# A recurrence whose response part runs ahead of its scan, and a gate product through split parts, on one core

## The reference, cut to what matters

```python
def step(x, u_blk):                      # of s5_scan; complex state x, 64 states in each of 64 groups
    bu = jnp.einsum('btgh,gph->btgp', u_blk.astype(jnp.complex64), b_bar)
    bu = bu.at[:, 0].add(a_bar * x)
    a = jnp.broadcast_to(a_bar, bu.shape)
    _, xs = lax.associative_scan(_affine_compose, (a, bu), axis=1)
    y = jnp.einsum('btgp,ghp->btgh', xs, c_mat).real
    return xs[:, -1], y
...
def s5_out(y, u, d_skip, w_glu, dtype):
    b, t = u.shape[:2]
    y = (y + d_skip.astype(jnp.float32).reshape(S5_GROUPS, S5_GROUP) * u).reshape(b, t, D_MODEL)
    z = jax.nn.gelu(y).astype(dtype) @ w_glu
    za, zb = jnp.split(z, 2, axis=-1)
    return za * jax.nn.sigmoid(zb)
...
    y_lf, _ = s5_scan(u_l, ab_f, bb_f, c_f, x_cf)
    y_lb, _ = s5_scan(u_l[:, ::-1], ab_b, bb_b, c_b, x_cb)
    out_l = s5_out(y_lf + y_lb[:, ::-1], u_l, d_skip, w_glu, h_l.dtype)
```

## Time and profile before

| | |
|---|---|
| median of 3 runs | 2630.1 us (2624.09, 2630.1, 2630.54) |
| profiled execution | 2623.83 us, span 2622.0 us, granted clock 0.962 |
| busy in the span | PE 2353.7 (90%), PEld 1857.2 (71%), DVE 1478.4 (56%), ACT 1035.9 (40%), POOL 210.2 (8%) |
| chain that ended last | PE 73%, DVE 14%, ACT 7%, DMA 3% |
| recurrence, from the norm's root to the first gate matmul | 2162 to 2356.4 |
| gate product | 2356.4 to 2413.5 |
| last norm, to the last MLP's first matmul | 2413.5 to 2429.7 |

### The profile page before, as it was taken

One profiled execution on the slowest core, in us unless ns is written; L12 is line 12 of the kernel. 1 busy time (PEld: TensorE's weight loads), 2 busy tenths in 40 slices (PEclk: granted clock), 3 DMA queues, 4 the chain that ended last, 5 costly groups with the idle time before them and its releaser, 6 DMA issues.

```text
span 2622.0 us, 35101 instructions
## 1 busy us (share of the span) xinstructions
PE 2353.7 (90%) x14706; PEld 1857.2 (71%) x14706; DVE 1478.4 (56%) x2327; ACT 1035.9 (40%) x1742; POOL 210.2 (8%) x294
## 2 busy tenths in 40 slices
PE   5987788999997988888997988989999998978999
PEld 2854365888884766667996853357788778757999
DVE  5337656556555377875455235546566545871454
ACT  3243444222234355554444335544322324221543
POOL 0001200000000033320000002200201100000110
PEclk8988999999998999998998999999999998989999
DMA  7145552434421455334552323423444332352453
GB/s 265 65 162 201 227 191 68 159 137 151 152 89 65 140 181 161 129 129 138 189 185 83 105 92 131 171 110 120 137 153 150 122 147 103 130 187 95 161 180 126
DMA packets 174846, 372.78 MB, mean 142 GB/s; under 512 B 8384, under 2 KB 101824, under 8 KB 160480
## 3 DMA queue, kind: packets, MB, share of 16 engines
q1 hardware_dynamic: 174688, 370.53, 40.3%
HBM read 340.07 MB, written 30.44 MB: 141 GB/s over the span
## 4 chain that ended last, share of the span: by engine, by line
PE 73%; DVE 14%; ACT 7%; DMA 3%; issue 2%; POOL 0%; SPq 0%; DVEq 0%; ACTq 0%
PE ps L169 72%; DVE sb_R L200 5%; ACT sb_R L248 2%; DMA sb_R<-mod_w 1%; DVE sb_R L232 1%; DVE sb_WP L200 1%; DMA sb_slot<-mod_w 1%; DVE sb_H L200 1%; PE ps L179 1%; DVE sb_cst L214 1%; DVE sb_X L217 1%; DVE sb_R L229 1%; DVE sb_cst L200 1%; ACT L244 1%; ACT sb_R L254 1%
## 5 line engine op out<-in xcount | busy, mean ns | idle before, releaser
L169 PE MATMUL ps<-sb_HP,sb_WP 128*128 128x512 f32 (+1 forms) x5736 | 1087.8, 351 | 48.6 <-DVE sb_WP L200 24.6
L169 PEld LDWEIGHTS ps<-sb_HP,sb_WP 128*128 128x128 f32 x5736 | 923.4, 192 | 196.9 <-DVE sb_HP L200 22.7
L200 DVE TENSOR_TENSOR sb_WP<-sb_slot,sb_WP 128x1024 fp32r<-128x1024 f32 x364 | 449.5, 1240 | 650.9 <-ACT sb_WP L254 650.7
L254 ACT ACTIVATE sb_WP<-sb_slot 128x1024 fp32r<-128x1024 f32 x364 | 383.0, 1057 | 788.9 <-PE ps L169 774.0
L169 PE MATMUL ps<-sb_XP,sb_WP 128*128 128x512 f32 (+1 forms) x2592 | 450.9, 336 | 10.2 <-DVE sb_XP L200 10.2
L169 PEld LDWEIGHTS ps<-sb_XP,sb_WP 128*128 128x128 f32 x2592 | 398.6, 190 | 62.6 <-DVE sb_XP L200 12.2
L200 POOL TENSOR_TENSOR sb_R<-sb_R 128x128 f32<-128x128 f32 (+2 forms) x194 | 155.6, 825 | 1809.2 <-ACT sb_R L248 1383.9
L169 PE MATMUL ps<-sb_R 128*32 128x64 f32 (+8 forms) x2088 | 169.2, 285 | 60.4 <-DVE sb_R L200 24.6
L200 DVE TENSOR_TENSOR sb_R<-sb_R 128x256 f32<-128x256 f32 (+3 forms) x398 | 201.0, 539 | 27.2 <-ACT sb_R L248 24.2
L169 PEld LDWEIGHTS ps<-sb_R 128*32 128x32 f32 (+5 forms) x2088 | 119.5, 149 | 118.0 <-issue 62.6
L248 ACT ACTIVATE sb_R<-ps 128x512 f32<-128x512 f32 (+1 forms) x208 | 99.4, 514 | 128.4 <-PE ps L169 124.9
(11 more groups left out here) (136 smaller groups left out, 1936.9 us busy)
## 6 DMA issues: line engine op xcount, KB each, us to landing
sb_slot<-mlp_w SPq DMA_DIRECT2D x32, 2048.0 KB, 9.0
sb_slot<-mod_w SPq DMA_DIRECT2D x22, 2048.0 KB, 8.9
sb_R<-ada_w SPq DMA_DIRECT2D x12, 2048.0 KB, 7.5
sb_slot<-ada_w SPq DMA_DIRECT2D x24, 1024.0 KB, 4.8
sb_slot<-ffn_w_gate SPq DMA_DIRECT2D x22, 1024.0 KB, 5.2
sb_slot<-ffn_w_up SPq DMA_DIRECT2D x22, 1024.0 KB, 7.8
sb_slot<-ffn_w_down SPq DMA_DIRECT2D x10, 2048.0 KB, 7.6
sb_slot<-odd_w_in SPq DMA_DIRECT2D x32, 512.0 KB, 7.2
```

The source lines that it names most:

```text
L169: return self.e.matmul(out, w, x, start=start, stop=stop, skip_group_check=True)
L200: return BLANK if self.e is None else self.e.tensor_tensor(out, a, b, op)
L254: return self.e.activation(out, a, ACT.Copy) if scale is None else self.e.activation(out, a, ACT.Copy, scale=scale)
```

## The change

1. ORDER: inputs 0 come ahead of response 0; response 3 comes directly behind response 2, ahead of outputs 2; collect 2 is split into an ACT copy to Y2 (ahead of scan 3) and an addition on DVE behind scan 3; the skip is taken on DVE before scan 3.
2. outputs_pe does the response part of all four f first, then waits for the scan once, then does the scan's part of all four.
3. LW has two buffers, W3 three, and CA of unit 3 has a place of its own (in slot 0, RS and the constants' area), loaded by four DMAs ahead of CA 2.
4. At the start ACT takes two of turn 0's copies before each of its four norm shifts; turn_pe waits for W3 only ahead of its last quarter.
5. The fences between recurrence and gate go; the gate matrix goes as 16 pieces through WP (slots 1, 2, 0, 3 in this order), gelu's result is split in gp, and PE uses mm3; each piece's four k tiles feed two outputs.
6. The gate stage splits the last MLP's first three pieces.

```diff
-    ORDER = ("response 0", "inputs 0", "turn 1", "inputs 1", "turn 2", "scan 0", "outputs 0", "collect 0", "inputs 2",
-             "response 1", "turn 3", "scan 1", "outputs 1", "collect 1", "inputs 3", "response 2", "scan 2",
-             "outputs 2", "response 3", "scan 3", "collect 2", "outputs 3", "collect 3")
+    ORDER = ("inputs 0", "response 0", "turn 1", "inputs 1", "turn 2", "scan 0", "outputs 0", "collect 0",
+             "inputs 2", "response 1", "turn 3", "scan 1", "outputs 1", "collect 1", "inputs 3", "response 2", "response 3", "scan 2",
+             "outputs 2", "collect 2", "skip 3", "scan 3", "add 2", "outputs 3", "collect 3")
...
+        self.LWflat = [p.slots[3][:, 0:2048], spare(2048)]
+        self.CA4 = [[self.CAflat[:, 2560 * i:2560 * i + 2048] for i in range(2)], [p.slots[0][:, 2048 * i:2048 * i + 2048] for i in range(2)]]
+        self.CA1 = [[self.CAflat[:, 2560 * i + 2048:2560 * i + 2560] for i in range(2)], [spare(512), p.RS[:, :]]]
...
-        self.W, self.W3 = p.slots[0][:, 0:3072], [p.slots[0][:, 3072:4096], place(1024)]
+        last = place(1024)
+        self.W, self.W3 = p.slots[0][:, 0:3072], [cst, p.slots[0][:, 3072:4096], last]
...
+        self.pieces = Pieces(p, "s5.glu", [self.glu_load(g) for g in range(4)], (1, 2, 0, 3))
+        self.pieces.free = self.place_free
...
+    def place_free(self, e, x):
+
+        e.wait_ge("y", 2, 3, of="s5.scan")
+        e.wait_ge("bu", 3, 3, 1, of="s5.scan")
...
-            if u >= 2:
-                e.wait_ge("turned", u - 2, 3, 1)
-                e.wait_ge("resp", u - 2, 3)
+            if u == 3:
+                e.wait_ge("turned", 0, 3, 1)
+                e.wait_ge("resp", 0, 3)
...
+        def load_last_CA():
+            e.wait_ge("turned", 3, 2, 1)
+            e.wait_ge("resp", 1, 3)
+            for i in range(2):
+                e.dma(self.CA4[1][i], params.CA[3][:, 2560 * i:2560 * i + 2048]).then_inc(*e.full("full_CA3", "CA4", i))
+                e.dma(self.CA1[1][i], params.CA[3][:, 2560 * i + 2048:2560 * i + 2560]).then_inc(*e.full("full_CA3", *("CA1", i) if i == 0 else ("CA", 3)))
...
-        for u in range(1, 4):
-            load_CA(u)
-            if u == 1:
-                load_W(3)
-            if u < 3:
-                load_P(u + 1)
+        load_P(2)
+        load_CA(1)
+        load_W(3)
+        load_P(3)
+        load_last_CA()
+        load_CA(2)
...
     def response_act(self, e, u):
-        if u:
-            e.wait_ge("y", u - 1, 3)
+        if u >= 2:
+            e.wait_ge("y", u - 2, 3)
...
             e.wait_ge("LW", u, f)
             for tau in range(4):
-                e.mm(o[:, tau:4, :], self.LW[:, f, tau, :], lat[:, 0:4 - tau, :], tau == 0, False)
-            e.wait_ge("scanned", u)
+                e.mm(o[:, tau:4, :], self.LW[u % 2][:, f, tau, :], lat[:, 0:4 - tau, :], tau == 0, False)
+        e.wait_ge("scanned", u)
+        for f, (b, o) in enumerate(outs):
             for s in range(4):
...
+        for y in range(16):
+            g, h = y // 4, y // 2 % 2
+            if y % 2 == 0:
+                bs = [e.take(4 * h, 4 * h + 4) for _ in range(2)]
+            e.wait_ge("w", y)
+            w = p.wp(y % 4)
+            for k in range(4 * (y % 2), 4 * (y % 2) + 4):
+                e.wait_ge("gp", k)
+                for x, (b, ps) in enumerate(bs):
+                    c = 256 * (k % 4) + 128 * x
+                    m = e.mm3(ps[:, 0:TC], [z[:, c:c + 128] for z in w], self.gp(k), k == 0, k == KT - 1)
...
     def act(self, act):
         p, e = self.p, act.on("s5.in")
-        self.norm.act(e)
-        self.turn_act(act.on("s5.scan"), 0)
+        self.norm.head_act(e)
+        self.mods.wait_co(e, 0)
+        turns = self.turn_act(act.on("s5.scan"), 0)
+        for t in range(1, KT, 2):
+            for _ in range(2):
+                next(turns)
+            self.norm.act_shift(e, t)
...
+        self.pieces.act_first(act)
         for f in range(8):
-            e.wait_ge("skip", f)
+            e.wait_ge("all", f, of="s5.scan")
             e.act(self.G[:, f, :], self.Y[:, f, :], ACT.Gelu_apprx_tanh).then_inc(*e.sig("g", f))
+            e.wait_ge("g", f)
+            e.copy(self.gp(f)[0], self.G[:, f, :]).then_inc(*e.sig("ghi", f))
...
+            if what == "add":
+                for k in range(4):
+                    self.glu_dve(g, k)
+                self.pieces.dve_part(g, 0)
+        for x in range(1, 3):
+            self.pieces.dve_part(g, x)
+        for k in range(4, 8):
+            self.glu_dve(g, k)
...
+        self.then.dve_first(dve)
...
-                                (mla.out.down, mlp0.pieces, mla.out.pieces)):
+                                (mla.out.down, mlp0.pieces, mla.out.pieces), (s5, mlp1.pieces, s5.pieces)):
```

More of the change, by code:

```diff
@@ L740, with __init__ @@
 class Pieces:
-    def __init__(self, p, name, loads):
+    def __init__(self, p, name, loads, slots=None):
         self.p, self.name, self.loads, self.list, self.prior, self.free = p, name, loads, [], None, None
+        self.slots = [n % 2 for n in range(len(loads))] if slots is None else slots
         for n, (size, _) in enumerate(loads):
@@ L757, in load @@
     def load(self, sp, n):
-        s, parts = n % 2, self.loads[n][1]
+        s, parts = self.slots[n], self.loads[n][1]
         sp.slot_free(s)
@@ L3507, in act, with glu_dve @@
                 self.response_act(e, int(u))
-            elif what == "collect" and int(u) < 2:
-                self.collect(e, int(u))
-        act.fence("s5.scan")
+            elif what == "collect" and int(u) < 3:
+                self.collect_act(e, int(u))
         e = act.on("s5.glu")
+        self.pieces.act_first(act)
         for f in range(8):
-            e.wait_ge("skip", f)
+            e.wait_ge("all", f, of="s5.scan")
             e.act(self.G[:, f, :], self.Y[:, f, :], ACT.Gelu_apprx_tanh).then_inc(*e.sig("g", f))
-        for x in range(8):
-            ps = e.wait_ge("zb", x)
-            if x >= 2:
-                e.wait_ge("o", x - 2)
-            e.act(self.sgm[x % 2], ps[:, 0:TC], ACT.Sigmoid).then_inc(*e.sig("sg", x))
-    def dve(self, dve):
-        p, e = self.p, dve.on("s5.in")
-        dve.on("s5.scan").fill(p.slots[3][:, 0:2048]).then_inc(*dve.on("s5.scan").sig("LW0"))
-        self.norm.dve(e)
-        e = dve.on("s5.scan")
+            e.wait_ge("g", f)
+            e.copy(self.gp(f)[0], self.G[:, f, :]).then_inc(*e.sig("ghi", f))
+        for g in range(4):
+            for y in range(4 * g, 4 * g + 4):
+                self.pieces.act_part(e, y + 3)
+            for x in (2 * g, 2 * g + 1):
+                ps = e.wait_ge("zb", x)
+                if x >= 2:
+                    e.wait_ge("o", x - 2)
+                e.act(self.sgm[x % 2], ps[:, 0:TC], ACT.Sigmoid).then_inc(*e.sig("sg", x))
+        self.then.act_first(act)
+    def glu_dve(self, e, k):
+        e.wait_ge("ghi", k)
+        hi, lo = self.gp(k)
+        e.sub(lo, self.G[:, k, :], hi.bitcast(F32)).then_inc(*e.sig("gp", k))
+    def dve(self, dve):
+        p, e = self.p, dve.on("s5.scan")
+        e.fence("1.prep")
+        for u in range(2):
+            e.fill(self.LWflat[u]).then_inc(*e.sig("LW0", u))
+        self.norm.dve(dve.on("s5.in"))
+        g = dve.on("s5.glu")
         for step in self.ORDER:
```

143 lines of the change are left out of this document (81 added, 62 removed).

## The result

The changed kernel takes 2585.96 us (median of 4 runs, 2583.73 to 2589.09) against 2629.56 for the kernel before beside it; the ratio is 0.9839, with a 95% interval from 0.9822 to 0.9856, so 38 to 47 us less (43.6 by the medians). 2590 was forecast, with a range from 2579 to 2606. Its profiled execution took 2585.31 us with a span of 2583.5 us.

The account below looks back on a forecast made before the run. PE and DVE were taken to bound the recurrence in turn, PE the last MLP. Gains of 24.0 (recurrence), 8.0 (gate) and 8.5 (norm) sum to 40.5 us: 2589.6 by the median, said as 2590, range 2579 to 2606.

Parts of the forecast that it names:

- y 3: The end of outputs 3 in the recurrence, forecast at 2329.2 instead of 2353.2, a gain of 24.0 us.
- the gate: Gate product as 384 f32r matmuls, 46.2 us plus 1.3 for the clock; a further gain of 8.0 us.
- the norm: Between gate and last MLP: with three pieces split ahead, PE starts sooner; gain 8.5 us, DVE margin 0.3 us.
- Start and middle: Recurrence up to scan 3: inputs 0 start 11.8 us earlier, and inputs 3's V copies end 12.4 us earlier.
- The giving back ahead of turn 1: Recurrence: ACT's V copies and 16 LW copies, 1.12 us a bank, hold up turn 1, losing part of the early start.
- End of the recurrence: Around scan 3: outputs 3's response part ends 1.8 us ahead of the scan, leaving only the scan's part behind it.
- only the scan's 4.2 us are left: Outputs 3 behind scan 3: four scan's parts at 1.04 us starts, 4.2 us in all.
- Its head: Gate start, set by DVE's chain: PE starts at 2331.9 on piece 0 and goes on at 2336.9 after gp 4.
- the formula: Rival in the gate: the page's issue gap holds, 109.2 instead of 120.3 ns a matmul, 2586 us; chance 0.04.
- Half clock in turns 1 and 3: Rival: half clock at ACT-paced places, 6.6 us a turn, about 11 together with outputs 3, 2601 us; chance 0.13.
- the rival of half clock throughout: Rival: PE at half clock from turn 0 to the gate's end, 109 us lost against 40, 2698 us; chance 0.02.
- the splits bind: Rival in the gate: each of 16 pieces lays 1.06 + 1.25 us bare, 37 us, 2627 us; chance 0.03.

Follow-up runs that it names:

- e8: The changed kernel with response 0 ahead of inputs 0 again; one run took 2583.76 us.
- e10: The changed kernel with response 0 moved behind turn 2 and response 1 behind turn 3, just ahead of their outputs; one run took 2584.5 us.
- e9: The changed kernel itself, run again without an edit; 2586.75 us, ratio 0.9857 to the kernel before.
- e6: The changed kernel, but in outputs 0 and 1 the scan's part of each f follows its response part; one run took 2585.92 us.
- e4: The changed kernel, but in outputs 3 alone the scan's part of each f follows its response part; 2589.18 us, ratio 0.9851.
- e7: The changed kernel, but the gate's second weight load (2 MB) waits for the end of outputs 3 instead of scan 3; one run took 2582.69 us.
- e11: The changed kernel with the edits of e10, e6 (here for outputs 0, 1 and 2) and e7 together; 2581.06 us, ratio 0.9828.
- e1: The changed kernel, but the last MLP's first three pieces are split after the norm again; 2593.98 us, ratio 0.9876.
- e5: The changed kernel, but each gate product leaves out its third matmul, 256 f32r matmuls instead of 384; one run took 2570.83 us.
- e2: The changed kernel with the recurrence's old order, ACT's turn 0 copies behind the norm, and scan's part behind each response part; 2597.32 us, ratio 0.988.
- e12: e11 with the subtractions of the gate's first three WP pieces on GpSimd beside scan 3 instead of on DVE; 2583.63 us, ratio 0.9841.

## Why the prediction was right

The 41.3 us come from the three places that were forecast, but not in the forecast's shares. From the ends of the rows above and of the kernel before: y 3 came 19.9 us earlier, where 24.0 stood in the sum; the gate gave 13.0, where 8.0 stood; the norm gave 8.4, where 8.5 stood. Two errors of 4 to 5 us cancel; how they hang together is told below.

**Start and middle**: each step came within 1.2 us of the forecast, inputs 0 by 0.6 and scan 3 by 0.5 early. The giving back ahead of turn 1, worked out from the pace of 1.12 us for a bank's LW copies, is confirmed by e8 (4.4 at the start, 0.8 at inputs 1) and by e10, where it is avoided. No moved DMA was waited for: no row of PE in this stretch names one, where the earlier trace rows has two.

**End of the recurrence.** The response part of outputs 3 was ready ahead of the scan as said, by 1.57 us where 1.8 stood. The step that failed is the next one, "only the scan's 4.2 us are left": from release to gate PE took 8.8. It rested on the small matmuls' price when mixed with longer ones; in a row they came at half clock (0.66 granted from the release to the pause) and with a pause. In e9 the clock was full up to the pause, and the pause was 4.47 instead of 2.80; it ended 7.8 us behind the release in both (2327.50 to 2335.27 and 2327.62 to 2335.45). In all eight traces that have the run and the early load it ended 7.8 to 8.7 us behind it. So PE's pace does not set this end. e6 and e4 show that the pause needs a run of small matmuls, e7 and e11 that it ends 2 to 4 us sooner when the weights don't move then.

**Gate.** Its head was forecast at 170.3, set by DVE's chain and not by y 3, with PE waiting 2.7 us for piece 0 and 2.1 more for gp 4. It started at 171.65 and waited for neither, because DVE was by then just ahead of it. So the late outputs (4.6 us) took the place of the waits (4.8 us): e7, which shortens the one, gets part of the other back, 0.60 and 1.74 us. That is why a term wrong by 4.6 us left only 1.3 at the gate's start and nothing at its end. That DVE's chain bounds the gate's head was in the forecast, so an end of outputs 3 without a pause would not have brought the gate much nearer; that the late end was just as long as the waits, and not longer, was luck. The product took 47.36 us with its half clock, where 46.2 + 1.3 was forecast. The Trainium skill (TensorE: Matmul & The Clock Gate, Back-to-back issue gap) gives the formula N / 2.4 + 2.5 for an isolated matmul, and says of streams of a weight load and a matmul that the two together set the pace. By the formula the estimate was 41.9 us; this stream took 123.3 ns each here and 120.3 in the earlier trace rows, where the Trainium skill's formula has 109.2.

**Norm.** 8.5 was forecast, and 8.4 is what e1 takes away; DVE's three subtractions (3.49) ended 0.9 us before the norm wanted DVE, more than the 0.3 that was worked out.

**Rivals.** Half clock in turns 1 and 3 did not come: turn 1 took 8.03 us and turn 3 7.9 from first to last row, with 1.00 granted in both. It came in the scan's part of outputs 3, where it wasn't looked for, and cost nothing, as the pause ended when it would; and at the gate's head, for which 1.3 us stood in the sum. The price of this rival was summed low: at its own 6.6 us a turn, two turns alone are 13, not 11. In the rival of half clock throughout, 0.213 less 0.120 for 384 is 36 us, not 37. That the splits bind fell by e5. On the total: the profiled execution was forecast at 2583.3 and took 2585.31, of which the 3.1 us of the unedited part explain more than all. The 2590 for the median stood 6.3 above the profiled execution, as in the kernel before; in the changed kernel the two lie 0.7 apart, which is scatter and not a part of the mechanism.

## What to carry to other kernels

Ask of a step that is moved forward what the engine then waits for next. Here inputs 0 started 12.4 us earlier; 4.4 of that came from the swap with response 0, and only 0.8 of these were left at inputs 1, until e10 moved the response's copies out of the way too. Work that can be done ahead of a long operation (here four response parts ahead of the scan) leaves the short pieces in one row, and their price in a row is not their price when mixed. When a forecast comes out right, compare its terms too: here two of them were off by 4 to 5 us in opposite directions. And when a helper engine is idle, look at what it shares with the one that is not, before giving it work.

## What the runs showed of the hardware

- **A pause inside a run of small matmuls.** 256 matmuls of 64 columns with 256 weight loads take about 4 us, and PE pauses 0.9 to 1.8 us in them in outputs 0 and 1 of every kernel that has them in a row, with nothing to wait for, and within a group of 64; mixed with response parts it never does (e2, e6, e11). Outputs 2 has the same run and no pause, except in e8, ahead of its last matmul: the pauses stand at fixed places of PE's program. With 2 MB in rows of 1 KB on the DMA queues the pause in outputs 3 was 2.80 to 4.94 us; with the load moved away 0.37 after half clock (e7), 1.08 at full clock (e11), and none in e12, where PE was at half clock nearly throughout.
- **What the pause waits for.** The traces have transfers of kind "instruction" of 16 KB (this is the one in the long pause of the changed kernel, DMA queues from 2332.5 to 2333.0):

```profile
q8 instruction: 1, 0.02, 14.2%
```

It starts at 2332.79, 5.3 us behind the release, and takes 1.1 us. Each of the 29 pauses ends 1.2 to 1.6 us behind the end of such a transfer, however long it lasts. In outputs 3 the transfer starts 2.1 to 2.8 us behind the release when the weights don't move (e7, e11, e12), and 5.2 to 6.3 when they do. In e12 it had ended before PE came to the place, and there is no pause. So the pause fits a wait for the next instructions, which the weights' load delays. No run changed these transfers alone, so the link rests on this timing.
- **GpSimd beside DVE.** Two-operand DVE multiplications of 128x1024 took 3.20 to 3.38 us each instead of 1.16 while GpSimd subtracted (3.3 us a piece); each ended 1.1 us, about its own length, behind a piece of GpSimd's. The two hardware scans, of which the last 2.3 us lay beside GpSimd's first piece, kept their 8.88 us, and it was that piece that was longer, 4.44 us. The Trainium skill, SBUF — State Buffer, Who interferes with whom, says that a DVE instruction with two SBUF inputs contends with a GpSimd instruction that reads SBUF, because its second input comes through the shared read interface; for the multiplications the trace agrees.
- **Clock.** In the scan's part of outputs 3 the granted clock was 0.59 from 2328 to 2330 in the changed kernel's trace, after 1.57 us of idleness, and 1.00 in e9 after 1.24. The length of the idle stretch does not decide it: e8 came back after 1.14 us at half clock (1.51 for 48 small matmuls), e6 after 2.13 at full (0.88). The two levels are 1.2 and 2.4 GHz; the same program gets either here.
- **Scatter.** The unedited first 2161 us ended up to 9.8 us apart between executions, more than most single steps of this change are worth. Counted from one common row, the same recurrence came out within 0.9 us in seven traces, so that one trace showed effects of 2 us and more which the repeated runs left open.
